# A hybrid decoder step on one Trainium2 core: expert 0 of each layer dispatched alone in the routing block, and one block from the experts to the attention values

## Chip, cores and metric

The kernel runs on one core of a Trainium2 chip, as one program and one launch. The metric is the device time of one execution in microseconds (us), the median of several. TensorE (PE in the profile) multiplies, PEld is its loading of stationary operands, VectorE is DVE, ScalarE is ACT, GpSimd is POOL, and SyncE is SP, which issues most of the transfers.

## The reference, cut to what matters

Two layers run over 264 tokens (256 of a prompt, 8 of a sample). Each has a mixer, then 32 experts of which every token uses two, then a gate term (PLE). After layer 0 the shared latents and rotary keys are computed from the same `h`.

```python
h = h + mixer(rmsnorm(h))                       # layer 0: convolution, layer 1: attention on the latents
x = rmsnorm(h)                                  # experts: top 2 of 32 by group and inner logits
hmid = silu(xblk @ w1[e]) * (xblk @ w3[e])      # w1, w3: 1024 x 512 each, float32
y[tokens] += (hmid @ w2[e]) * gate              # w2: 512 x 1024
h = h + sigmoid(rmsnorm(h) @ w_gate + b) * (p[i] @ w_proj)
# after layer 0 only
u = rmsnorm(h); c = rmsnorm(u @ w_dkv); k_pe = rope(u @ w_kr)
# layer 1's mixer
cq = rmsnorm(rmsnorm(h) @ w_dq); q = cq @ w_uq; k = c @ w_uk; v = c @ w_uv
```

All is float32. An expert's weights are 6 MiB (4 MiB for w1 and w3, which the kernel calls "up", and 2 MiB for w2, "down"); both layers together load 384 MiB of them.

## The kernel before, in words

`h` is held transposed as `hT` (8 chunks of 128 features by 264 tokens). The engines' programs are written out by hand, block by block; at the end of a block (`nc.Block()`) every engine waits for all others. Inside a block only semaphores order the work, and each engine runs its list in order.

`route_stage` (line 1033) is one block. It computes the logits, picks the experts, turns the tokens' rows into `u_rows` (tokens by features), counts ranks, and makes `sel`, one-hot columns that say which token sits in which slot. An expert has 32 slots. PE runs `busy`, products whose result nobody reads, where it would be idle. Then `dispatched` multiplies `u_rows` by `sel`, two feature chunks at a time (f = 0 to 3), which gives the inputs of experts 0 to 3 at once, transposed, and ACT copies them out with the gain (`dispatch_copy`).

`experts_stage` (line 1371) is the next block. It runs 36 turns, one for an expert (four experts have two). In turn e PE runs `expert_up` (line 1012, 32 products in four column groups), ACT the silu, DVE the product and a transpose (`turn_hidden`), PE `expert_down`, then ACT and DVE copy the result to `y`. Beside the turns stand the dispatch for the next eight turns (`fill_at`), `widen` (line 1541 on), `combine`, and from turn 32 on `project` of the PLE term. DVE has, ahead of turn 0, some 5 us of placing arithmetic (lines 1779 to 1809). The last combination, `combine_strips`, ends with eight additions to `hT`, from which ACT makes the eight gained chunks `uT`.

The weights lie in `area`: three up slots (`UPS`) and two down slots (`DOWNS`). Up slots 0 and 1 and both down slots are loaded long before; slot 2 at the start of `route_stage` (`first_up`). SP issues the up load of expert 3 once `up_done` of turn 0 is counted, that of expert 4 after turn 1, and so on; POOL issues nearly all down loads after `down_done`. From expert 4 on SP first reads the expert's number from memory (`expert_at`, line 1409).

`ple_stage` (line 1936) is the block after the experts. For each of 8 output chunks PE runs eight products of `uT` with the gate weights (line 1964) into PSUM banks 0 and 1 by turns; from chunk 2 on it waits for `scaled` of two chunks before. DVE needs the root of the sum of squares (lines 2046 to 2053) before it can scale. In layer 0 the next two blocks are `chunked` (line 2161) parts of `mla_stage` (line 2215): the latents, the rotary key and the down query, then keys, queries and values. In layer 1 `ple_stage` is the end, with turned rows (`followed`) between the products.

## Time and profile before

| | us |
|---|---|
| median of 3 runs (range) | 1435.5 (1432.87 to 1437.76) |
| the profiled execution, its own time | 1436.19 |
| its span in the trace | 1434.5 |
| PE busy | 1152.4 |
| DVE busy | 509.4 |
| ACT busy | 315.7 |

The times of rows below count from the start of the span; 1.7 us lie outside it. A row of the order in time gives start, duration, engine, line, operation, and in brackets how long the engine had been idle and what released it. Of a float32 product the trace counts two instructions.

### The profile page before, as it was taken

Reading aid. Unit: us, or ns where it says so; the run is one execution under the profiler, and the core shown is the slowest. Engines: PE = TensorE matmul, PEld = TensorE weight load, DVE = VectorE, ACT = ScalarE, POOL = GpSimd, SP = SyncE. Lnnn points to the kernel's source line nnn. Section 1 sums busy time; section 2 is a strip of 40 time slices with the busy share of each in tenths; the row PEclk is TensorE's granted clock in tenths of the full one; section 3 lists DMA queues with packets and bytes.
Section 4 is the critical chain, followed back from the end, with each engine's and each line's share of the span. In section 5 each row is a group of like instructions: output and inputs, shape, how many; then the busy total and the mean of one; then the engine's idle time right before and its main releaser. Section 6 shows DMA issues by size and latency. Waiting matters only on the chain. (4 is left out here: it accounts for less than half of the span.)

```text
span 1434.5 us, 25593 instructions
## 1 busy us (share of the span) xinstructions
PE 1152.4 (80%) x10905; PEld 726.7 (51%) x10905; DVE 509.4 (36%) x1421; ACT 315.7 (22%) x790; POOL 57.8 (4%) x84
## 2 busy tenths in 40 slices
PE   8999896857669676889989889997956958776687
PEld 7767653524325333467756557654533524333356
DVE  4873612212213121254856562522212212122144
ACT  4564320101101010142223330331100101101133
POOL 0200000000000000000011100000000000000000
PEclk9999997979879788999999999998988978889989
DMA  9453399999999999993033336679999999999970
GB/s 330 157 224 162 130 426 426 426 426 426 428 427 426 427 426 426 425 334 137 0 141 133 140 126 251 248 301 427 426 426 428 426 427 427 425 428 425 421 293 31
DMA packets 60235, 464.12 MB, mean 324 GB/s; under 512 B 17628, under 2 KB 28921, under 8 KB 33470
## 3 DMA queue, kind: packets, MB, share of 16 engines
q1 hardware_dynamic: 50974, 338.09, 57.6%
q0 software_dynamic: 8992, 123.74, 20.7%
q8 instruction: 90, 1.47, 0.4%
q10 hardware_dynamic: 144, 0.52, 0.1%
q14 instruction: 35, 0.29, 0.1%
HBM read 460.80 MB, written 2.49 MB: 323 GB/s over the span
## 5 line engine op out<-in xcount | busy, mean ns | idle before, releaser
L1018 PE MATMUL ps<-area,uT 128*32 128x256 f32 x2560 | 176.9, 437 | 95.7 <-DMA area<-in_w_exp_up_dram 93.5
L1018 PE MATMUL ps<-area,xsT 128*32 128x256 f32 x2048 | 152.7, 464 | 97.8 <-DMA area<-in_w_exp_up_dram 97.8
L1818 DVE TENSOR_TENSOR hidden<-silu,ps 128x128 f32<-128x128 f32 x72 | 20.7, 287 | 484.5 <-ACT silu L1678 484.5
L1018 PEld LDWEIGHTS ps<-area,uT 128*32 128x32 f32 x2560 | 91.7, 125 | 177.4 <-DMA area<-in_w_exp_up_dram 103.0
L1028 PE MATMUL ps<-area,hiddenT 128*32 128x256 f32 x2304 | 147.0, 398 | 26.0 <-issue 19.2
L1018 PEld LDWEIGHTS ps<-area,xsT 128*32 128x32 f32 x2048 | 76.1, 133 | 173.1 <-DMA area<-in_w_exp_up_dram 107.7
L1725 DVE COPY y<-ps 32x256 f32<-32x256 f32 x140 | 58.3, 416 | 192.8 <-PE ps L1028 191.0
L1349 PE MATMUL ps<-sel,u_rows 128*128 128x256 f32 (+3 forms) x480 | 124.6, 386 | 0.3
L1678 ACT ACTIVATE silu<-ps 128x128 f32<-128x128 f32 x72 | 20.0, 277 | 472.4 <-PE ps L1018 472.4
L1028 PEld LDWEIGHTS ps<-area,hiddenT 128*32 128x32 f32 x2304 | 71.6, 113 | 90.6 <-issue 37.2
L1349 PEld LDWEIGHTS ps<-sel,u_rows 128*128 128x128 f32 (+1 forms) x480 | 77.1, 187 | 44.5 <-issue 34.3
L1662 ACT COPY y<-ps 32x256 f32<-32x256 f32 x140 | 51.0, 365 | 159.2 <-PE ps L1028 158.3
L1526 PE MATMUL ps<-share,y 128*128 128x264 f32 (+1 forms) x288 | 83.9, 413 | 2.0 <-DVE hT L1708 1.5
L1964 PE MATMUL ps<-uT,area 128*128 128x264 f32 x256 | 63.2, 408 | 7.4 <-PEq L1453 7.4
L1526 PEld LDWEIGHTS ps<-share,y 128*128 128x128 f32 (+1 forms) x288 | 48.1, 189 | 37.3 <-issue 25.5
L320 PE MATMUL ps<-const,area 128*128 128x128 f32 (+2 forms) x356 | 55.3, 288 | 13.1 <-DVE cacheT L332 7.7
L1000 POOL DMA_DIRECT2D area<-in_w_exp_down_dram x50 | 26.7, 534 | 857.1 <-issue 644.8
L1964 PEld LDWEIGHTS ps<-uT,area 128*128 128x128 f32 x256 | 51.3, 203 | 17.6 <-issue 8.2
L1708 DVE TENSOR_TENSOR hT<-ps,hT 128x264 f32<-128x264 f32 x144 | 53.8, 409 | 5.7 <-PE ps L1526 5.6
L320 PEld LDWEIGHTS ps<-const,area 128*128 128x128 f32 (+2 forms) x356 | 40.7, 146 | 26.9 <-DVE cacheT L332 10.7
L590 PE MATMUL ps<-uT,area 128*128 128x264 f32 x160 | 36.6, 388 | 0.9 <-DVE conv_acc_sb L773 0.9
L590 PEld LDWEIGHTS ps<-uT,area 128*128 128x128 f32 x160 | 30.1, 190 | 6.7 <-DVE conv_acc_sb L773 1.3
(409 smaller groups left out, 1291.0 us busy)
## 6 DMA issues: line engine op xcount, KB each, us to landing
area<-in_w_exp_gate_dram SPq DMA_DIRECT2D x64, 2048.0 KB, 26.7
area<-in_w_exp_up_dram SPq DMA_DIRECT2D x64, 2048.0 KB, 33.6
area<-in_w_exp_down_dram POOLq DMA_DIRECT2D x50, 2048.0 KB, 15.3
area<-in_w_exp_down_dram SPq DMA_DIRECT2D x14, 2048.0 KB, 22.5
area<-in_conv_w_in_dram SPq DMA_DIRECT2D x8, 1024.0 KB, 21.5
area<-in_w_ple_gate_dram SPq DMA_DIRECT2D x8, 1024.0 KB, 20.8
area<-in_conv_w_out_dram SPq DMA_DIRECT2D x1, 4096.0 KB, 26.2
area<-in_w_o_dram SPq DMA_DIRECT2D x1, 4096.0 KB, 14.4
```

The lines of the kernel that those rows point to most:

```text
L320: last = pe.transpose(s.ps[0:m, 8 - banks + g % banks, at:at + n], src, col(s, "ident", slice(0, n))[:, 0:n])
L590: done = pe.matmul(s.ps[:, pair(m) + half, 0:T], w_in[:, k, a:a + P], s.uT[:, k, :], start=(k == 0), stop=(k == DC - 1))
L1000: engine.dma_start(down_view(s, slot).rearrange("p j d -> p (j d)"), src.rearrange("a p n -> (a p) n"))\
L1018: last = pe.matmul(s.ps[SLOT * j:SLOT * (j + 1), bank, 0:2 * P].rearrange("p (a f) -> p a f", a=2), xT[:, k, :], up[:, :, k, j * P:(j + 1) ...
L1028: last = pe.matmul(s.ps[SLOT * g:SLOT * (g + 1), bank, 0:q], hidden[:, SLOT * j:SLOT * (j + 1)], down[:, j, g * q:(g + 1) * q], start=(j = ...
L1349: last = pe.matmul(s.ps[:, bank, (c % 2) * WIDE + at:(c % 2 + 1) * WIDE], rows_of(m, t, c), m.sel[0:rows, t, at:WIDE], start=(t == 0), sto ...
L1526: pe.matmul(s.ps[:, 6 + c % 2, 0:T], y[0:rows, quad % 2, c * P:(c + 1) * P], share[0:rows, 0, :], start=True, stop=True).then_inc(s.comb_m ...
L1662: last = nc.scalar.copy(y[a:a + SLOT, (e // PER) % 2, g * q4:(g + 1) * q4], s.ps[SLOT * g:SLOT * (g + 1), 3 + e % 2, 0:q4])
L1708: V.tensor_tensor(s.hT[:, c, :], s.ps[:, 6 + c % 2, 0:T], s.hT[:, c, :], ALU.add)\
L1725: last = V.tensor_copy(y[a:a + SLOT, (e // PER) % 2, g * q4:(g + 1) * q4], s.ps[SLOT * g:SLOT * (g + 1), 3 + e % 2, 0:q4])
L1818: V.tensor_tensor(hid[:], act_out[:], s.ps[:, e % 2, P:2 * P], ALU.mult).then_inc(s.gated.sem, 1)
L1964: mm = pe.matmul(s.ps[:, c % 2, 0:T], w[:, k, c * P:(c + 1) * P], s.uT[:, k, :], start=(k == 0), stop=(k == DC - 1))
```

## The change

- **Expert 0 alone.** In `route_stage` DVE makes the 32 columns of `sel` for expert 0 first, then the other 96. PE multiplies them with `first_rows` (12 products in four column groups: rows of the slot by features), runs two fillers, and DVE transposes the result in 32 x 32 blocks and applies the gain. PE then runs `expert_up` of expert 0 in this block. SP waits there for it and issues the up load of expert 3. Only f = 0 of the dispatch of experts 1 to 3 (96 columns) is left in the block.
- **The first turns.** f = 1, 2 and 3 move to turn 0 of `experts_stage`; the dispatch for the next eight turns moves from turns 0 to 3 to `begun`, a turn or half a turn later. DVE's placing arithmetic now stands behind its first transpose, and its copy of turn 0 ahead of `choose(1)`.
- **One block.** `experts_stage`, `ple_stage` and, in layer 0, both `chunked` parts stand in one block. The barriers between them go, and waits on counts take their place. SP waits for the last `up_done` before the loads of attention weights, and for the end of the gate products before w_o.
- **Gate products.** They take the chunks of `uT` in the order in which these come, waiting for each, and use banks 0, 1, 5 and 7 (in layer 1 the second four use 0, 1, 0, 1). The product of the sum of squares moves from behind chunk 0 to behind chunk 1. `combine_strips` uses banks 2 to 7, so its last two products wait for an addition.
- **Latents.** Behind the last gate product PE runs seven of the eight products each for both latent chunks, the last sum of squares, and seven for the rotary key; the eighth of each follows once the last chunk is gained.
- Counters are merged (`conv_set`, `prepared`).

```diff
@@ route_stage
+                sp.wait_ge(s.up_done.sem, s.up_done.at(1))
+                first_up(sp, s, io, layer, UPS)
...
                 busy(pe, 2)
+                pe.wait_ge(s.first_sel.sem, s.first_sel.at(1))
+                first_rows(pe, s, m, 4).then_inc(s.first_mm.sem, 1)
+                busy(pe, 2)
+                pe.wait_ge(s.up_in[0].sem, s.up_in[0].at(32))
+                pe.wait_ge(s.first_out.sem, s.first_out.at(1))
+                expert_up(pe, s, up_view(s, 0), first_inputs(s)[:, :, P:P + SLOT], 0).then_inc(s.up_done.sem, 1)
                 pe.wait_ge(s.sel_ready.sem, s.sel_ready.at(1))
-                for f in range(DC // 2):
-                    if f >= 2:
-                        pe.wait_ge(s.xs_out.sem, s.xs_out.at(f - 1))
-                    dispatched(pe, s, m, f, 5 + f % 2, P).then_inc(s.xs_mm.sem, 1)
+                dispatched(pe, s, m, 0, 5, P + SLOT).then_inc(s.xs_mm.sem, 1)
...
+                own = first_inputs(s)[:, :, P:P + SLOT]
+                dve.wait_ge(s.first_mm.sem, s.first_mm.at(1))
+                link(V.transpose(own, s.ps[:, 4, 0:DC * SLOT].rearrange("p (k m) -> p k m", k=DC)))
+                V.tensor_tensor(own, own, s.gain[:, layer, :].rearrange("p (k a) -> p k a", a=1)
+                                .broadcast_to([P, DC, SLOT]), ALU.mult).then_inc(s.first_out.sem, 1)
@@ experts_stage
+        begun = {0: ((), ()), 1: ((), (0,)), 2: ((1,), (2,)), 3: ((3,), ())}
...
+            def dispatch_rest(f):
+                if f >= 2:
+                    pe.wait_ge(s.xs_out.sem, s.xs_out.at(f - 1))
+                dispatched(pe, s, m, f, 5 + f % 2, P + SLOT).then_inc(s.xs_mm.sem, 1)
...
-                for p in range(UPS, CUT):
+            for p in range(UPS + 1, CUT):
@@ ple_stage
+    banks = (0, 1, 5, 7, 0, 1, 0, 1) if last else (0, 1, 5, 7) * 2
...
+            for n, (k, gained) in enumerate(m.gained):
+                if c == 0:
+                    pe.wait_ge(s.gained.sem, gained)
+                mm = pe.matmul(s.ps[:, banks[c], 0:T], w[:, k, c * P:(c + 1) * P], s.uT[:, k, :],
+                               start=(n == 0), stop=(n == DC - 1))
@@ mla_stage
+            for b, (weights, a) in enumerate(firsts):
+                if weights is w.kr:
+                    last_sum(pe)
+                    pe.wait_ge(s.prepared.sem, s.prepared.at(1))
+                for k in range(DC - 1):
...
+            return "job", last_product, raw_result(raw, c)
```

Three places of PE's list follow; a name in brackets is a counter that the instruction waits for. The first is the end of `route_stage` and the start of the experts' block in layer 0. L1094 are fillers, L1349 the dispatch, L1018 the up products. Before:

```order
L1094 MATMUL ps<-hT,ones 128x264
L1349 MATMUL ps<-sel,u_rows 128x128 [waits sel_ready]
L1349 MATMUL ps<-sel,u_rows 128x128 x11
L1349 MATMUL ps<-sel,u_rows 128x128 [waits xs_out]
L1349 MATMUL ps<-sel,u_rows 128x128 x5
L1349 MATMUL ps<-sel,u_rows 128x128 [waits xs_out]
L1349 MATMUL ps<-sel,u_rows 128x128 x5
L1096 UNCONDITIONAL_BRANCH
L1507 UNCONDITIONAL_BRANCH [waits barrier_Pool_Activation_PE_DVE_SP_release]
L1018 MATMUL ps<-area,uT 32x256 [waits xs_out,up_in0]
```

After (L1375 is `first_rows`, L1364 the dispatch, L1028 the down products):

```order
L1094 MATMUL ps<-hT,ones 128x264
L1375 MATMUL ps<-u_rows,sel 32x256 [waits first_sel]
L1375 MATMUL ps<-u_rows,sel 32x256 x11
L1094 MATMUL ps<-hT,ones 128x264 x2
L1018 MATMUL ps<-area,uT 32x256 [waits first_out,up_in0]
L1018 MATMUL ps<-area,uT 32x256 x31
L1364 MATMUL ps<-sel,u_rows 128x96 [waits sel_ready]
L1364 MATMUL ps<-sel,u_rows 128x96 x5
L1096 UNCONDITIONAL_BRANCH
L1532 UNCONDITIONAL_BRANCH [waits barrier_Pool_Activation_PE_DVE_SP_release]
L1364 MATMUL ps<-sel,u_rows 128x96 x6
L1028 MATMUL ps<-area,hiddenT 32x256 [waits down_in0,h_ready]
```

The up products of expert 0 moved from behind 24 dispatch products and the barrier to ahead of both; eighteen of the dispatch products moved behind the barrier.

The second place is the end of layer 0's experts and the first gate products. Before (L1538 are the strips, L1964 the gate products, L1969 the sum of squares):

```order
L1538 MATMUL ps<-more_share,y 128x264 x7
L1453 UNCONDITIONAL_BRANCH
L1956 UNCONDITIONAL_BRANCH [waits barrier_Pool_Activation_PE_DVE_SP_release]
L1964 MATMUL ps<-uT,area 128x264 [waits ple_in0]
L1964 MATMUL ps<-uT,area 128x264 x7
L1969 MATMUL ps<-rstd,ones 128x264 [waits summed]
L1964 MATMUL ps<-uT,area 128x264 x8
L1964 MATMUL ps<-uT,area 128x264 [waits scaled,ple_in1]
```

After:

```order
L1570 MATMUL ps<-more_share,y 128x264 x5
L1570 MATMUL ps<-more_share,y 128x264 [waits added] x2
L2017 UNCONDITIONAL_BRANCH
L2027 MATMUL ps<-uT,area 128x264 [waits gained,ple_in0]
L2027 MATMUL ps<-uT,area 128x264 [waits gained] x7
L2027 MATMUL ps<-uT,area 128x264 x8
L2032 MATMUL ps<-rstd,ones 128x264 [waits summed]
L2027 MATMUL ps<-uT,area 128x264 [waits ple_in1]
L2027 MATMUL ps<-uT,area 128x264 x15
L2027 MATMUL ps<-uT,area 128x264 [waits scaled,ple_in2]
```

The barrier is gone, the products of chunk 0 wait for one gained chunk each, and two more chunks stand ahead of the first wait for `scaled`.

The third place is from the last gate products to the down query. Before (L2157 are the latents, the rotary key with 64 rows, and the down query):

```order
L1969 MATMUL ps<-area,ones 128x264 [waits summed]
L1969 MATMUL ps<-area,ones 128x264 [waits squared]
L1952 UNCONDITIONAL_BRANCH
L2181 UNCONDITIONAL_BRANCH [waits barrier_Pool_Activation_PE_DVE_SP_release]
L2157 MATMUL ps<-area 128x264 [waits attn_in0]
L2157 MATMUL ps<-area 128x264 x15
L2157 MATMUL ps<-area 64x264 [waits swapped]
L2157 MATMUL ps<-area 64x264 x7
L2157 MATMUL ps<-area 128x264 [waits proj_out,attn_in1]
```

After:

```order
L2409 MATMUL ps<-area 128x264 [waits gained,attn_in0,scaled]
L2409 MATMUL ps<-area 128x264 [waits gained] x6
L2409 MATMUL ps<-area 128x264 x7
L2394 MATMUL ps<-area,ones 128x264 [waits summed]
L2396 MATMUL ps<-area,ones 128x264 [waits squared]
L2409 MATMUL ps<-area 64x264 [waits prepared]
L2409 MATMUL ps<-area 64x264 x6
L2416 MATMUL ps<-area 128x264 [waits gained]
L2416 MATMUL ps<-area 128x264
L2416 MATMUL ps<-area 64x264
L2224 MATMUL ps<-area 128x264 [waits proj_out,attn_in1]
```

Fourteen products now stand ahead of the last sum of squares, and no barrier between.

## Rows read from the trace of the kernel before

**Rows 1.** The page, 40 slices: DMA's busy share in tenths, and GB/s

```profile
DMA  9453399999999999993033336679999999999970
GB/s 330 157 224 162 130 426 426 426 426 426 428 427 426 427 426 426 425 334 137 0 141 133 140 126 251 248 301 427 426 426 428 426 427 427 425 428 425 421 293 31
```

**Rows 2.** Who SP waited for: total us, times, longest

```profile
SPq L1409 <- PE ps L1018: 616.6, 48, 24.4
```

**Rows 3.** Order in time, layer 0: the end of routing and turn 0

```profile
160.60 1.13 PE L1094 MATMUL ps<-hT,ones 128*128 128x264 f32 x4 [0.99 <-ACT u_rows L1087]
...
161.57 8.49 PE L1349 MATMUL ps<-sel,u_rows 128*128 128x128 f32 x48
...
171.18 5.35 PE L1018 MATMUL ps<-area,uT 128*32 128x256 f32 x64 [1.12 <-PEq L1096]
...
176.58 0.33 SPq L994 DMA_DIRECT2D area<-in_w_exp_gate_dram  x1
...
177.22 0.41 DVE L1364 STREAM_TRANSPOSE hiddenT<-hidden 128x128 f32<-128x128 f32 x1
```

**Rows 4.** The same list in layer 1: the same load of expert 3

```profile
941.26 0.33 SPq L994 DMA_DIRECT2D area<-in_w_exp_gate_dram  x1
```

**Rows 5.** Two stretches: length, engines' busy us, granted clock, DMA share, GB/s

```profile
172.00:173.00 1.00, 1.00 (x19) 0.65 (x12) 0.83 (x6) 0.28 (x1) 0.00 (x0) 0.52 0.00 0
...
176.00:180.00 4.00, 2.72 (x45) 1.24 (x37) 3.31 (x12) 2.14 (x8) 0.04 (x1) 1.00 0.63 172
```

**Rows 6.** Order in time, layer 0: turns 0 and 1

```profile
177.68 1.93 PE L1028 MATMUL ps<-area,hiddenT 128*32 128x256 f32 x32 [1.15 <-DVE hiddenT L1364]
...
183.11 3.66 PE L1018 MATMUL ps<-area,uT 128*32 128x256 f32 x64
...
187.83 0.36 SPq L994 DMA_DIRECT2D area<-in_w_exp_gate_dram  x1
```

**Rows 7.** Order in time, layer 0: the last turns, the gate, the latents

```profile
596.65 6.34 PE L1018 MATMUL ps<-area,uT 128*32 128x256 f32 x64 [3.37 <-DMA area<-in_w_exp_up_dram]
...
619.89 1.17 PE L1538 MATMUL ps<-more_share,y 32*128 32x264 f32 x16 [0.54 <-DVE y L1721]
...
621.11 3.35 ACT L1699 ACTIVATE uT<-hT,vec 128x264 f32<-128x264 f32 x8 [1.32 <-DVE hT L1840]
...
624.77 6.10 PE L1964 MATMUL ps<-uT,area 128*128 128x264 f32 x16 [3.71 <-PEq L1453]
...
631.15 25.08 PE L1964 MATMUL ps<-uT,area 128*128 128x264 f32 x112
...
659.88 16.51 PE L2157 MATMUL ps<-area 128*128 128x264 f32 x64 [0.32 <-PEq L1952]
```

**Rows 8.** The first load of gate weights: issue, and time from issue to landing

```profile
L1920 SPq DMA_DIRECT2D area<-in_w_ple_gate_dram x1: 435/435/435, 591.7 to 591.7; - x1
...
DMA to landing us min/median/max: 27.4/27.4/27.4
```

**Rows 9.** Order in time, layer 0: the second sum, the latent norm, the first keys

```profile
658.85 0.71 PE L1969 MATMUL ps<-area,ones 128*128 128x264 f32 x2 [0.57 <-DVE area L2040]
...
676.23 1.05 PE L391 MATMUL ps<-latent_squares,ones 128*128 128x264 f32 x4
...
685.20 1.97 PE L2157 MATMUL ps<-cT,area 128*128 128x256 f32 x8 [0.79 <-PEq L2167]
```

**Rows 10.** Order in time, layer 1: the gate products of the end

```profile
1389.41 6.07 PE L1964 MATMUL ps<-uT,area 128*128 128x264 f32 x16 [3.71 <-PEq L1453]
...
1390.70 3.13 DVE L2046 TENSOR_TENSOR rstd<-rstd,area 128x264 f32<-128x264 f32 x6
...
1398.31 0.43 DVE L2053 TENSOR_TENSOR xsT<-ps,rstd 128x264 f32<-128x264 f32 x1
...
1400.26 0.52 ACT L2017 ACTIVATE area<-hT,vec 128x264 f32<-128x264 f32 x1 [0.97 <-DVE hT L2064]
...
1402.88 0.38 PE L1973 MATMUL ps<-const,area 128*128 128x128 f32 x2
```

More of the change, by code:

```diff
@@ L1351, in dispatched, with first_rows @@
     return last
+def first_rows(pe, s, m, bank):
+    for t, (_, rows) in enumerate(TILES):
+        for g in range(PER):
+            src = m.u_rows[0:rows, t, :].rearrange("t (k p) -> t k p", k=DC)[:, :, SLOT * g:SLOT * (g + 1)]
+            out = s.ps[SLOT * g:SLOT * (g + 1), bank, 0:DC * SLOT].rearrange("p (k m) -> p k m", k=DC)
+            last = pe.matmul(out, m.sel[0:rows, t, P:P + SLOT], src, start=(t == 0), stop=(t == 2))
+    return last
 def dispatch_copy(copy, s, layer, xT, f, bank, at=0):
```

1173 lines of the change are left out of this document (615 added, 558 removed).

## The prediction

> **What bounds the kernel now.** I read the page first. The slices of DMA show two long stretches near full (5 to 17 and 27 to 37 of 40) with a nearly empty stretch before each [rows 1]. Those are the experts. SP waited 616.6 us there in 48 waits for up products to free a slot [rows 2]; the slots are full, and behind them stands a queue of transfers. The last but one load of up weights still makes PE wait, at 596.65 [rows 7]. So each experts' stage lasts as long as its transfers, counted from their first issue, and that issue is what counts: SP may ask for expert 3 only when PE ends the up products of turn 0, at 176.58 in layer 0 [rows 3] and 941.26 in layer 1 [rows 4]. No transfer of weights runs before it. Around the experts PE's chain sets the time: 8 gate products of eight, the latents, the queries.
>
> **First part: the load of expert 3 is issued earlier.** PE's fillers before the dispatch end at 160.60 + 1.13 = 161.73 [rows 3]; the selection of expert 0 is a part of the old one and is ready by then. From there the new path is:
> - `first_rows`, 12 products in groups of four. Turn 1's up products, 32 of the same shape, take 3.66 us [rows 6], so a group of four takes 0.46, and 12 take 1.37: to 163.1.
> - DVE's transpose of 256 columns: 128 columns take 0.41 [rows 3], so between 0.41 and 0.82; I take 0.55. The multiplication by the gain is like the 0.43 of [rows 10]. With some 0.2 for hand-overs the inputs stand at 164.3. Two fillers (half of 1.13, 0.6 to 1.1 with their start) hide part of it from PE's clock.
> - the up products at the full clock, 3.66: to 168.0, and the issue at 168.05.
>
> That is 8.5 us before 176.58. DVE's waits and two operations (2.9 us in all) stand ahead of the rest of its routing arithmetic, but ACT's copy of the dispatch ends the block before: PE dispatches f = 0 now until about 170.1, as f = 3 before (161.57 + 8.49 = 170.06 [rows 3]), so the next block still starts near 171.2.
>
> **What comes late next** is the load of expert 4, issued after turn 1's up products. Ahead of these PE has, from 171.2: the dispatch f = 1, turn 0's down products (1.93 [rows 6]), f = 2 and 3, and turn 1's 3.66. A dispatch of 128 columns costs 8.49 / 4 = 2.12 [rows 3]; with 96 columns at least three quarters of that, 1.59, at most all; I take 1.9. Sum 5.7 + 1.93 + 3.66 + 0.3 of waits = 11.6: to 182.8. In before PE's clock was granted at half (0.52 in 172 to 173 [rows 5]), after the barrier's 1.12 us of idling, and turn 0 took 5.35 instead of 3.66. That barrier stays, so I add the same 1.7: to 184.5. SP issues 1.06 after the products' end, since it must read the expert's number (183.11 + 3.66 = 186.77 against 187.83 [rows 6]): 185.6.
> The transfers ahead of it are expert 3 up (4 MiB) and a down load (2 MiB), 6.29 MB. After the issue at 176.58 the stretch 176 to 180 moved 4.0 us x 172 GB/s = 0.69 MB, 1.6 us at the 426 GB/s of the page's slices [rows 1]; so data flow 1.8 after the issue [rows 5]. The queue is then empty at 168.05 + 1.8 + 14.8 = 184.65, and expert 4 flows from 187.4. **The hole is 2.75**, and 1.05 without the low clock. Later issues come before the queue runs dry (expert 5's near 196.9, when expert 4 and a down load keep it until 202.3). So a layer's experts end 8.5 - 2.75 = 5.75 earlier, and two layers give **11.5** (bounds: a hole of 4 each, 9.0; a hole of 1.05, 14.9). DVE's placing arithmetic, now behind turn 0's transpose, ends near 179; the next reader of `sel` for turns 4 on needs it at 188.
>
> On the clock: the row shows the level fall to 1.2 GHz after a gap of 1.12 us [rows 3, 5]. The Trainium skill, "TensorE: Matmul & The Clock Gate", section "Loop structure matters more than you think", says that a short copy by DVE between batches of products doesn't cost the clock. By that rule the hole would be 1.05 and the two layers would give 14.9; by the row 11.5. I keep the row.
>
> **The gate in layer 0.** PE idled 3.71 from the strips to 624.77, and the first 8 products took 6.10 where later ones take 25.08 / 7 = 3.58 [rows 7]. Now they may start with the first gained chunk, at 621.11 + 0.42 + 0.1 = 621.65; ACT makes a chunk in 0.42, PE needs 0.45 for a product, so PE is not held up. The weights land at 591.7 + 27.4 = 619.1, 2.5 before [rows 8] (both move with the stream). Eight chunks and the sum at full clock: 8 x 3.58 + 0.7 = 29.3, to 651.0, against 631.15 + 25.08 = 656.23 [rows 7]: 5.2. With as much low clock as before, 2.5 less. No wait for `scaled` bites, since four banks let PE run ahead of the root. The strips' last two products wait for an addition each, 0.5 us later, hidden by DVE's own eight additions. I take **4.4** (2.7 to 5.2).
>
> **The latents.** From the end of the gate to the end of the first down query took 676.23 - 656.23 = 20.0 [rows 7, 9]. Now: 14 products at 0.448 (6.3), the sum (0.7, its last square is ready at 656.23 - 651.0 before 658.85, so at 653.6), 7 and 3 products (4.5), 8 of the down query (3.6), waits 0.4: 15.5. That gives 4.5. The root (two hand-overs and DVE's reciprocal) hides behind the rotary key's seven. The barrier before the keys goes too, and DVE's apply then limits them: 0.7 more. **5.2** (3.0 to 6.3; the low end if ACT's and DVE's results follow as late as before).
>
> **The gate in layer 1.** Here the rows of the result need the gained chunk 0, so the root counts. The running sum is ready at 1390.70 + 3.13 = 1393.83; PE made its product only behind the first, slow chunk, 1389.41 + 6.07 = 1395.48 [rows 10]. Now it comes at 1393.9 at the earliest, 1.6 sooner, and chunk 0 is gained at 1400.26 + 0.52 - 1.6 = 1399.2, when the turned rows go out, instead of 1402.88: 3.7. With a low clock in the first chunk the sum waits for PE again, and 2.2 is left. I take **2.9** (1 to 3.7).
>
> **The sum.** 11.5 + 4.4 + 5.2 + 2.9 = 24.0. The profiled execution took 1436.19, 0.7 above the median of the runs; 1436.2 - 24.0 = 1412.2, and in terms of the median 1411.5.
>
> **The rivals.**
> - The clock holds at turn 0 in both layers, and at the gate. For it: two fillers and the early up products keep PE busy to 168. Against: the same barrier stands behind the dispatch [rows 3, 5]. 14.9 + 5.2 + 5.2 + 3.7 = 29.0: 1406.5. Chance 0.22.
> - The start is given back. PE is the slower one in turns 0 to 4, and the queue could run dry again at turn 2 or 3, until only the old schedule is left; that decides if expert 5's load is issued after 202.3, 5.4 later than I put it. The stream then gives nothing: 24.0 - 11.5 = 12.5, 1423.0. Chance 0.08.
> - The merged blocks don't do what they say, since ACT and DVE, not PE, set the pace of gate and latents: 7 less, 1418.5. The rows with PE without a pause for 25.08 us speak against. Chance 0.05.
> - Slower: PE, waiting chunk by chunk for ACT, stays at half clock in the gates. A chunk then costs 6.10 instead of 3.58 [rows 7]; all 16 cost 16 x 2.5 = 40, time 1411.5 + 40 = 1451.5, and from ten such chunks on the change loses. Against it: today only the first chunk of eight is slow, and the second already costs 3.58. Chance 0.03.
> - Gains under 4.3 us for causes I don't see: 0.02.
>
> **How the numbers follow.** My forecast, 1411.5, has 0.60. The range takes in the clock that holds, both ends of the unknown costs, and the slower merged blocks, but not the stream that gives all back: 1404 to 1420. A measurement of this kernel tells 0.3% (4.3 us) from no change. All cases but the last two are faster by more: faster 0.95, same 0.02, slower 0.03.
>
> **What would show it.** In the changed profile: the load of expert 3 issued at 168.05 in layer 0, 8.5 earlier; a dip of DMA of about 3 us, some 17 after it; expert 4's issue near 185.6; the gate products starting 0.5 after the first gained chunk; no idle PE between gate and latents. I am wrong if the clock doesn't fall behind the barrier, if `first_rows` doesn't run four at a time (1.37 would be up to 5.5, and the stream lose 4 per layer), or if the queue has a second dip.

## The result, and the profile after

The changed kernel takes 1418.85 us in the median of four runs (1414.27 to 1424.74), the kernel before 1434.87; the ratio is 0.9879, 95% interval 0.9848 to 0.9911. Measured once more (e1) it is 1419.68 in six runs (1408.75 to 1423.67), ratio 0.9886 (0.9850 to 0.9922). The forecast was 1411.5, in a range of 1404 to 1420: the sign and the range hold, but the gain is 16, not 24. The profiled execution was the longest of the four, 1424.74 with a span of 1423.1; the profiled one of e1 took 1418.4 (span 1416.6) and lies near the median, so both are used.

The page of the changed kernel, DMA's busy share and GB/s (to be set beside [rows 1]):

```profile
DMA  9454589999999999994034427589999999999980
GB/s 331 159 218 172 199 362 427 426 427 426 427 427 424 428 426 424 426 332 181 1 142 143 152 108 287 223 321 426 427 427 426 426 426 427 426 427 425 426 306 31
```

The slice ahead of the first experts' weights, the fifth, had 130 GB/s and now has 199, and the next one has 362 where it had 426: weights flow earlier, and then stop for a while. In slices 25 to 27 of the second layer it is 287, 223, 321, where before had 251, 248, 301.

Order in time, layer 0, from expert 0's own inputs to the load of expert 4 (beside [rows 3] and [rows 6]):

```profile
163.00 1.64 PE L1375 MATMUL ps<-u_rows,sel 128*32 128x256 f32 x24
...
164.70 0.45 DVE L1262 STREAM_TRANSPOSE uT<-ps 128x256 f32<-128x256 f32 x1 [0.96 <-PE ps L1375]
165.18 0.42 DVE L1263 TENSOR_TENSOR uT<-uT,gain 128x256 f32<-128x256 f32 x1
...
165.75 3.66 PE L1018 MATMUL ps<-area,uT 128*32 128x256 f32 x64
...
169.34 2.07 PE L1364 MATMUL ps<-sel,u_rows 128*128 128x96 f32 x12
169.46 0.33 SPq L994 DMA_DIRECT2D area<-in_w_exp_gate_dram  x1
...
172.33 3.21 PE L1364 MATMUL ps<-sel,u_rows 128*128 128x96 f32 x12 [0.92 <-PEq L1096]
...
175.47 3.64 PE L1028 MATMUL ps<-area,hiddenT 128*32 128x256 f32 x32
...
179.04 4.54 PE L1364 MATMUL ps<-sel,u_rows 128*128 128x96 f32 x24
...
183.51 5.05 PE L1018 MATMUL ps<-area,uT 128*32 128x256 f32 x64
...
189.64 0.36 SPq L994 DMA_DIRECT2D area<-in_w_exp_gate_dram  x1
```

Down to the load of expert 3 the intervals are as forecast: it is issued 17.96 us after that of slot 2 (151.50), against 26.42 before, 8.46 earlier. Then PE is slow. The down products take 3.64 instead of 1.93, turn 1's up products 5.05 instead of 3.66, and expert 4's load comes 20.2 after expert 3's, where I had put 17.6. (The trace holds two entries for each of these products; counts here are of entries.) The windows of that stretch (length, busy us of PE, PEld, DVE, ACT, POOL, granted clock, DMA share, GB/s):

```profile
172.00:174.00 2.00, 1.67 (x7) 1.35 (x8) 0.10 (x1) 1.59 (x3) 0.00 (x0) 0.68 0.96 410
174.00:178.00 4.00, 4.00 (x30) 2.31 (x33) 3.59 (x16) 2.10 (x8) 0.00 (x0) 0.50 1.00 430
...
180.00:182.00 2.00, 2.00 (x13) 1.62 (x13) 0.54 (x2) 0.57 (x2) 0.18 (x1) 1.00 0.99 352
...
183.00:186.00 3.00, 3.00 (x26) 1.53 (x30) 2.15 (x6) 0.57 (x2) 0.00 (x0) 0.50 0.98 393
...
188.00:190.00 2.00, 2.00 (x22) 1.42 (x14) 0.69 (x2) 0.28 (x1) 0.00 (x0) 1.00 0.04 16
```

The clock falls twice. The first fall, at the barrier's pause, was forecast. The second comes at 183, while PE has worked without a pause since 172.3: what it did just ahead of it were the dispatch products of 96 columns. At 188 to 190 no weights flow (16 GB/s): that is the hole. In layer 1 the level stays at 1.2 GHz from 926.5 to 944:

```profile
926.00 2.74 PE L1364 MATMUL ps<-sel,u_rows 128*128 128x96 f32 x12 [0.92 <-PEq L1096]
928.67 3.64 PE L1028 MATMUL ps<-area,hiddenT 128*32 128x256 f32 x32
932.24 7.14 PE L1364 MATMUL ps<-sel,u_rows 128*128 128x96 f32 x24
939.31 6.03 PE L1018 MATMUL ps<-area,uT 128*32 128x256 f32 x64
```

and expert 4's load comes 23.2 after expert 3's.

The gate and the latents in layer 0 (beside [rows 7] and [rows 9]):

```profile
617.22 2.28 PE L1570 MATMUL ps<-more_share,y 32*128 32x264 f32 x16 [0.54 <-DVE y L1767]
619.42 9.07 PE L2027 MATMUL ps<-uT,area 128*128 128x264 f32 x32
628.34 0.61 PE L2032 MATMUL ps<-rstd,ones 128*128 128x264 f32 x2
628.78 21.52 PE L2027 MATMUL ps<-uT,area 128*128 128x264 f32 x96
650.14 6.39 PE L2409 MATMUL ps<-area 128*128 128x264 f32 x28
...
665.95 1.05 PE L391 MATMUL ps<-latent_squares,ones 128*128 128x264 f32 x4
```

PE has no pause in it, the first gate product follows right on the strips, 1.0 behind the start of the first gained chunk (618.43), and from the gate's end (650.30) to the sum of the latents' squares it is 15.65 instead of 20.0.

**Where the time is.** The span cut at the same ten marks, one profiled execution of each kernel, in us. "Stream" is from the issue of expert 3's load to the start of the last down products. It is 440.1 to 440.9 in the kernels below whose transfers do not stop once they flow (before, e7, e9).

| stretch | before | after | e1 | e3 | e6 | e7 | e9 | e8 |
|---|---|---|---|---|---|---|---|---|
| start to slot 2's load, layer 0 | 150.16 | 151.50 | 151.86 | 150.13 | 152.26 | 151.99 | 150.38 | 150.45 |
| to expert 3's load | 26.42 | 17.96 | 17.96 | 17.96 | 17.97 | 18.35 | 26.27 | 17.97 |
| stream, layer 0 | 440.84 | 445.28 | 445.33 | 444.08 | 443.29 | 440.15 | 440.85 | 442.22 |
| strips to the gate's end | 36.34 | 33.08 | 33.09 | 31.40 | 31.40 | 31.40 | 31.40 | 31.40 |
| gate's end to the queries' products | 39.94 | 34.67 | 34.73 | 34.63 | 34.56 | 34.71 | 34.55 | 39.24 |
| to slot 2's load, layer 1 | 218.68 | 220.20 | 219.27 | 220.33 | 223.09 | 223.51 | 220.24 | 218.01 |
| to expert 3's load | 26.41 | 17.96 | 17.97 | 17.97 | 17.97 | 18.35 | 24.74 | 17.97 |
| stream, layer 1 | 440.79 | 449.34 | 443.29 | 443.99 | 441.58 | 440.13 | 440.44 | 442.80 |
| strips to the end, layer 1 | 49.97 | 48.15 | 48.15 | 46.49 | 46.45 | 46.49 | 46.08 | 47.80 |
| span (with 2.5 twice from last down to strips) | 1434.5 | 1423.1 | 1416.6 | 1411.9 | 1413.5 | 1410.0 | 1419.9 | 1412.8 |

The width of the hole can be read from the bytes. In the 20 us that begin 10 us behind the issue of expert 3's load the kernel before moves 428 GB/s, in layer 0 and much the same in layer 1 (430); a full slice of its page has 426. Less than that in the same stretch, turned into time, is the hole:

| layers 0 and 1 | after | e1 | e3 | e6 | e7 | e8 |
|---|---|---|---|---|---|---|
| GB/s | 313, 245 | 311, 375 | 333, 339 | 384, 390 | 421, 418 | 378, 380 |
| hole, us | 5.3, 8.5 | 5.4, 2.4 | 4.4, 4.1 | 2.0, 1.7 | 0.2, 0.4 | 2.3, 2.2 |
| expert 3's load to expert 4's | 20.2, 23.2 | 20.2, 17.2 | 19.0, 18.9 | 16.6, 16.5 | 7.3, 7.3 | 17.1, 17.0 |

In every column but e7's, where the second load comes in time, the hole is 14.6 to 14.9 less than the time between the two loads. The stream rows differ from these by up to 1.1, as PE's clock at the last turns is in them too.

The first and the sixth row, whose work the change leaves as it was, differ by up to 2.1 and 5.5 between the kernels; for instance 16 products at L856 took 5.40 in the changed kernel and 3.83 in before. Before has nearly the shortest of both, but e8, which is the changed kernel in both stretches, has 150.45 and 218.01: the difference belongs to the single execution, and it makes a single pair of profiles uncertain by some us. Single runs of the changed kernel spread over 16 us (ten runs), those of e3 over 3 (six), those of the kernel before over 12 (23 runs beside e1).

### The profile page after: what moved, and what is told of

It reads as the page before. It is cut to its first block and busy times, and to the rows that moved or that the text cites. A ratio compares the mean times of both kernels' runs of the same rounds, so it can differ in the third digit from the quotient of the medians.

```text
span 1423.1 us, 25682 instructions
## 1 busy us (share of the span) xinstructions
PE 1170.9 (82%) x10961; PEld 739.8 (52%) x10961; DVE 512.0 (36%) x1437; ACT 315.0 (22%) x790; POOL 58.0 (4%) x84
## 5 line engine op out<-in xcount | busy, mean ns | idle before, releaser
L1018 PE MATMUL ps<-area,uT 128*32 128x256 f32 x2560 | 182.9, 447 | 96.2 <-DMA area<-in_w_exp_up_dram 93.8
L1018 PE MATMUL ps<-area,xsT 128*32 128x256 f32 x2048 | 147.3, 451 | 87.0 <-DMA area<-in_w_exp_up_dram 87.0
L1018 PEld LDWEIGHTS ps<-area,uT 128*32 128x32 f32 x2560 | 92.1, 128 | 183.1 <-DMA area<-in_w_exp_up_dram 102.9
L1028 PE MATMUL ps<-area,hiddenT 128*32 128x256 f32 x2304 | 148.5, 401 | 18.4 <-issue 13.7
L1018 PEld LDWEIGHTS ps<-area,xsT 128*32 128x32 f32 x2048 | 75.2, 129 | 156.8 <-DMA area<-in_w_exp_up_dram 95.4
L1364 PE MATMUL ps<-sel,u_rows 128*128 128x256 f32 (+3 forms) x480 | 129.3, 398 | 1.8 <-PEq L1096 1.8
L1028 PEld LDWEIGHTS ps<-area,hiddenT 128*32 128x32 f32 x2304 | 71.7, 114 | 84.6 <-issue 33.9
L1364 PEld LDWEIGHTS ps<-sel,u_rows 128*128 128x128 f32 (+1 forms) x480 | 81.3, 198 | 47.8 <-issue 41.6
L2027 PEld LDWEIGHTS ps<-uT,area 128*128 128x128 f32 x256 | 50.3, 199 | 9.8 <-issue 0.7
```

The costliest lines, as they stand in the source:

```text
L1018: last = pe.matmul(s.ps[SLOT * j:SLOT * (j + 1), bank, 0:2 * P].rearrange("p (a f) -> p a f", a=2), xT[:, k, :], up[:, :, k, j * P:(j + 1) ...
L1028: last = pe.matmul(s.ps[SLOT * g:SLOT * (g + 1), bank, 0:q], hidden[:, SLOT * j:SLOT * (j + 1)], down[:, j, g * q:(g + 1) * q], start=(j = ...
L1364: last = pe.matmul(s.ps[:, bank, (c % 2) * WIDE + at:(c % 2 + 1) * WIDE], rows_of(m, t, c), m.sel[0:rows, t, at:WIDE], start=(t == 0), sto ...
L2027: mm = pe.matmul(s.ps[:, banks[c], 0:T], w[:, k, c * P:(c + 1) * P], s.uT[:, k, :], start=(n == 0), stop=(n == DC - 1))
```

## The experiments

The theories. The hole in the stream is what part one loses. **A**: it is as wide as it is since products of 96 columns hold PE at half clock. **B**: the pause at the barrier does it. **C**: it differs with the single execution.

**e1: the changed kernel again**, no edit.

> The changed kernel once more, nothing edited. Its first profile came from the slowest of four executions (1424.7 of 1414.3 to 1424.7), and there the clock was granted at half for 14 of the first 15 us of turns 0 and 1 in layer 1 (926.5 to 944) and for about 11 in layer 0. Theory A (the half clock follows from what PE executes there, products of 96 columns): the long half clock returns in this profile, expert 4's load is again issued 19 to 24 us after expert 3's in both layers, and the median stays at 1416 to 1421. Theory C (it is a matter of the single execution): another profile shows half clock for 4 us or less behind the barrier, expert 4's load 17 to 18 us after expert 3's, and a time of 1414 or less for that execution.

Measured: 1419.68. Layer 0 is the same to 0.05 us (20.18 between the loads, stream 445.33). In layer 1 the level was low for some 3 us only (the down products took 3.36, turn 1's up products 3.66) and the loads came 17.18 apart, stream 443.29 instead of 449.34. So C has a part: the same code costs 6 us more in one execution than in another. Even so a hole of 2.4 remains.

**e3: the dispatch at its full width.**

```diff
-                dispatched(pe, s, m, f, 5 + f % 2, P + SLOT).then_inc(s.xs_mm.sem, 1)
+                dispatched(pe, s, m, f, 5 + f % 2, P).then_inc(s.xs_mm.sem, 1)
...
-                dispatched(pe, s, m, 0, 5, P + SLOT).then_inc(s.xs_mm.sem, 1)
+                dispatched(pe, s, m, 0, 5, P).then_inc(s.xs_mm.sem, 1)
```

> One size changed: the dispatch products of experts 1 to 3 take all 128 columns of the group, not 96 (the 32 more are computed and not copied). Theory A (products of 96 columns behind weights of 128 keep PE at half clock or throw it back there, with no pause of PE needed): the second fall of the clock (at 183 in layer 0) goes away, the level returns to full within 4 us of the barrier in both layers, expert 4's load comes 16.5 to 18 us after expert 3's instead of 20.2 and 23.2, and the kernel is 4 to 9 us faster than the changed one. Theory B (the 0.92 us pause at the barrier and the waits for ACT's copies behind it do it): nothing changes, within 2 us of the changed kernel, half clock as long as in it. At full clock the wider products cost at most 0.005 us each more (8.49/48 = 0.177 against 2.07/12 = 0.173).

Measured: 1415.02 (1413.64 to 1416.74), ratio 0.9864 (0.9839 to 0.9889), 4.7 less than e1 on the same chip, though the two intervals overlap. PE in layer 0, behind the barrier:

```profile
171.07 3.09 PE L1364 MATMUL ps<-sel,u_rows 128*128 128x128 f32 x12 [0.92 <-PEq L1096]
174.09 3.64 PE L1028 MATMUL ps<-area,hiddenT 128*32 128x256 f32 x32
177.66 4.80 PE L1364 MATMUL ps<-sel,u_rows 128*128 128x128 f32 x24
182.39 3.66 PE L1018 MATMUL ps<-area,uT 128*32 128x256 f32 x64
```

The second fall is gone (3.66, not 5.05); the first is there still (3.09, 3.64). The loads are 19.0 and 18.9 apart, not the 16.5 to 18 expected, so A could be right on the second fall alone. The wider products cost next to nothing: 2.18 for 12 against 2.07.

But e8, described below, has the same narrow dispatch as the changed kernel, and its profile has no second fall either:

```profile
171.29 2.32 PE L1364 MATMUL ps<-sel,u_rows 128*128 128x96 f32 x12 [0.92 <-PEq L1096]
173.63 3.24 PE L1028 MATMUL ps<-area,hiddenT 128*32 128x256 f32 x32
176.80 4.08 PE L1364 MATMUL ps<-sel,u_rows 128*128 128x96 f32 x24
180.81 3.66 PE L1018 MATMUL ps<-area,uT 128*32 128x256 f32 x64
```

In its layer 1 it is the same (4.08, 3.66). So of the six layers profiled with 96 columns (after, e1, e8) three had turn 1's up products slow, and of the six with 128 columns behind one early expert (e3, e6, e11) none. That speaks for A and does not prove it: with so few layers C could do as much. The gate was faster by 1.7 in each layer of e3: its first 32 products take 7.39 where the changed kernel had 9.07 in both profiles and both layers. That is not the dispatch's width either: e8's layer 0 has 7.39 with 96 columns, and e5's layer 1 has 9.07 with 128. What the level does at the gate is open.

**e4: 96 columns in the kernel before.** In the routing block's dispatch `P` becomes `P + SLOT`, the columns of expert 0 are not computed.

> The kernel before with the 48 dispatch products of its routing block cut from 128 columns to 96; the columns of expert 0 are left out, so its inputs are not computed. No pause, wait or barrier is added. Theory A: the level falls to half inside these products, which ran at the full level for 8.5 us in before, and they take 10 to 16 us; the kernel is 2 to 8 us per layer slower, though it computes less. Theory B: the level stays full, the products take 8.2 to 8.4, and the time is within 2 us of before.

Measured: 1443.12 (1439.11 to 1445.73), ratio 1.0055 (1.0038 to 1.0073): a quarter of the dispatch left out makes the kernel slower. Expert 0's inputs are then missing, so what follows computes with other values. The 48 products took 14.04 in layer 0 and 11.13 in layer 1, against 8.49. In layer 1, where the level was full at their start (the windows' seventh number is the clock):

```profile
931.82 11.13 PE L1349 MATMUL ps<-sel,u_rows 128*128 128x96 f32 x48
...
934.00:936.00 2.00, 2.00 (x13) 1.62 (x13) 1.83 (x11) 0.62 (x3) 0.00 (x0) 0.94 0.00 0
936.00:938.00 2.00, 2.00 (x8) 1.66 (x9) 1.40 (x7) 0.54 (x2) 0.00 (x0) 0.50 0.00 0
```

PE has no pause from 931.8 on, and its level falls at 936. In before the 48 products of 128 columns ran at 2.4 GHz from first to last. That shows A's mechanism by itself. In layer 0 the level had fallen ahead of them, at 161, and did not come back in 14 us of such products. In layer 0 of e9 the level fell at the same place, and behind it stood the 128 columns:

```profile
160.82 2.06 PE L1094 MATMUL ps<-hT,ones 128*128 128x264 f32 x4 [0.99 <-ACT u_rows L1087]
162.67 9.14 PE L1348 MATMUL ps<-sel,u_rows 128*128 128x128 f32 x48
172.93 3.66 PE L1018 MATMUL ps<-area,uT 128*32 128x256 f32 x64 [1.12 <-PEq L1096]
```

There the level was back at 165, and the 48 cost 9.14. So the width matters; by e8 it does not decide every time.

**e6: fillers at the barrier**, on e3.

```diff
                 dispatched(pe, s, m, 0, 5, P).then_inc(s.xs_mm.sem, 1)
+                busy(pe, 2)
```

> e3_wide_rest with two filler products behind the last dispatch of the routing block, so that PE works while ACT copies and the barrier comes: its pause shrinks from 0.92 us to about 0.4. Theory B1 (the pause at the barrier starts the low clock): the level stays full behind the barrier, turn 0's down products take 1.93 instead of 3.64, expert 4's load comes 15.5 to 16.5 us after expert 3's instead of 19.0, and the kernel is 4 to 7 us faster than e3. Rival (the fall comes anyway, from the dispatch products or from the change of work): half clock behind the barrier as in e3, same time within 2 us.

Measured: 1413.50 (1410.76 to 1415.31), ratio 0.9840 (0.9816 to 0.9865).

```profile
173.68 2.15 PE L1365 MATMUL ps<-sel,u_rows 128*128 128x128 f32 x12 [0.30 <-PEq L1096]
176.02 1.93 PE L1028 MATMUL ps<-area,hiddenT 128*32 128x256 f32 x32 [0.19 <-DVE hiddenT L1390]
177.89 4.29 PE L1365 MATMUL ps<-sel,u_rows 128*128 128x128 f32 x24
182.11 3.66 PE L1018 MATMUL ps<-area,uT 128*32 128x256 f32 x64
```

B holds for the first fall: with a pause of 0.30 instead of 0.92 the level stays at 2.4 GHz, and the loads come 16.6 apart. It is so in all six layers with these fillers (e6, e10, e12), and in all ten with the pause of 0.92 (after, e1, e3, e8, e11) the level fell behind it. The fillers both shorten the pause and put wide products ahead of it; which of the two keeps the level isn't told apart. The time moved only 1.5 from e3, within the spread, where I had expected 4 to 7. The hole did get 2.4 narrower in both layers, by the bytes. In e6's profile this is lost again elsewhere: 4.9 in the first and sixth rows, and 1.7 in layer 0's last up products, which ran at half clock (5.35) and so are in its stream row. The rule of the Trainium skill, "TensorE: Matmul & The Clock Gate", section "Loop structure matters more than you think", which I had set against this row, speaks of a copy by VectorE between batches of products. The wait of 0.19 for VectorE's transpose, through which the level stayed, agrees with it; the 0.92 at the barrier lies outside it.

**e7: experts 0 and 1 both alone**, on e3. Three places of it:

```diff
-                first = select(nc, s, m.sel[:, :, P:P + SLOT], early_rel, 0, P)
+                first = select(nc, s, m.sel[:, :, P:P + 2 * SLOT], early_rel, 0, P)
...
                 first_rows(pe, s, m, 4).then_inc(s.first_mm.sem, 1)
-                busy(pe, 2)
+                first_rows(pe, s, m, 7, 1).then_inc(s.first_mm.sem, 1)
...
                 expert_up(pe, s, up_view(s, 0), first_inputs(s)[:, :, P:P + SLOT], 0).then_inc(s.up_done.sem, 1)
+                pe.wait_ge(s.up_in[1].sem, s.up_in[1].at(32))
+                pe.wait_ge(s.first_out.sem, s.first_out.at(2))
+                expert_up(pe, s, up_view(s, 1), first_inputs(s)[:, :, P + SLOT:P + 2 * SLOT], 1).then_inc(s.up_done.sem, 1)
...
-        begun = {0: ((), ()), 1: ((), (0,)), 2: ((1,), (2,)), 3: ((3,), ())}
+        begun = {0: ((), ()), 1: ((), ()), 2: ((0,), (1,)), 3: ((2,), (3,))}
```

> A candidate on top of e3_wide_rest: experts 0 and 1 are both dispatched alone with products of four a time (the second 24 take the place of the two fillers) and both have their up products ahead of the barrier; the first dispatch products of the second group stand behind turn 2's up products, not turn 1's down. If the hole in the stream of weights is what keeps part one from its gain (5.5 and 6.4 us without transfers in the first profile, some 4 in e3), expert 4's load now comes 7 to 9 us after expert 3's, the hole behind expert 3 is gone in both layers, and the kernel is 5 to 9 us faster than e3, 1406 to 1410. If the stream then runs dry one turn later (expert 5's load more than 25 us after expert 3's), the gain is 0 to 3.

Measured: 1408.00 (1406.67 to 1411.92), ratio 0.9810 (0.9785 to 0.9835). It beats both kernels of the case.

```profile
163.49 3.20 PE L1381 MATMUL ps<-u_rows,sel 128*32 128x256 f32 x48
166.62 7.11 PE L1018 MATMUL ps<-area,uT 128*32 128x256 f32 x128
...
176.70 3.53 PE L1370 MATMUL ps<-sel,u_rows 128*128 128x128 f32 x12 [0.86 <-PEq L1096]
```

Expert 4's load is issued 7.3 after expert 3's, and the stream is 440.15 and 440.13: no hole to speak of, though the clock falls at the barrier as before (3.53 for 12 products) and expert 5's load comes 21 later. With the queue full PE's clock in turns 0 to 2 costs nothing. That shows that part one lost most of its gain in the hole.

**e2, e5 and e9: part one undone, three times.** e9 is part two alone; e2 and e5 are on the way to it and failed to be that, each by the place of one piece of VectorE's work. e2 puts the dispatch of experts 0 to 3 back in front of the barrier, with the up products of expert 0 in turn 0:

```diff
-                pe.wait_ge(s.first_sel.sem, s.first_sel.at(1))
-                first_rows(pe, s, m, 4).then_inc(s.first_mm.sem, 1)
...
+                for f in range(DC // 2):
...
+                    dispatched(pe, s, m, f, 5 + f % 2, P).then_inc(s.xs_mm.sem, 1)
```

> The first part undone in the changed kernel: expert 0 is dispatched with experts 1 to 3 again (48 products of 128 columns ahead of the barrier, up products of expert 0 in turn 0, load of expert 3 behind them). All that concerns gate, latents and keys stays changed. As predicted blind (part one is worth 11.5): 11 to 12 us slower than the changed kernel, near 1430. By the profile of the changed kernel (stream gained 4.0 in layer 0 and nothing in layer 1): 3 to 6 us slower, 1422 to 1425, and only 10 to 13 faster than before, all of it from gates and latents.

Measured: 1438.24 (1431.71 to 1445.34), ratio 1.0026 (1.0004 to 1.0048), slower than before. Both forecasts missed, since the undoing was not clean: `place()` stood behind turn 0's transpose, where the changed kernel has it, and the selection of the next group behind that.

> As e2_group_of_four, with one thing more: VectorE computes the places of the tokens in front of turn 0's work, beside its up products, as in the kernel before, so that the selection for the second group doesn't come late. In e2 PE waited 6.10 us for that selection behind turn 0's down products and was at half clock after it. Expected: that wait is gone, expert 4's load comes some 11 us after expert 3's as in before (e2: 21.5), and what is left is part two alone. By the rows of the first profile (gate 3.2, latents and keys 5.3, gate of layer 1 1.8) 10 us faster than before, 1424; by the blind numbers 12.5, 1422. If e2's loss had another cause, it stays near 1438.

Measured: 1432.45 (1427.82 to 1438.30), ratio 0.9986 (0.9968 to 1.0004). `place()` was in front again, but the selection still behind the copy of turn 0's outputs. The first dispatch of the next group, in e2 and in e5:

```profile
184.15 6.37 PE L1348 MATMUL ps<-sel,u_rows 128*128 128x256 f32 x12 [6.10 <-DVE sel L1320]
```

```profile
184.38 6.38 PE L1348 MATMUL ps<-sel,u_rows 128*128 128x256 f32 x12 [3.06 <-DVE sel L1320]
```

A wait of 6.10 or 3.06 for VectorE, and both times half clock behind it (6.37 for 3.44), with expert 4's load 21.5 and 18.8 behind expert 3's.

```diff
-                    copy_out(0)
                     choose(1)
+                    copy_out(0)
```

> As e5_part_two_alone with one order mended: behind turn 0 VectorE makes the selection of the second group before it copies turn 0's outputs, as in the kernel before (in e5 it came behind the copy and PE waited 3.06 us for it, then ran the next dispatch at half clock, 6.38 for 3.44). This is now part two alone. Expected: expert 4's load 11.2 us after expert 3's as in before, stretch from expert 3's load to the last down products 440.8 us as in before, and a time of 1423 to 1425 (10.4 to 12.5 less than before). Part one is then worth 3 to 6 as it stands in the changed kernel (1419). Rival: part two costs something in the experts' stage itself (merged block, placing arithmetic), and the time stays at 1430 or more.

Measured: 1422.83 (1418.15 to 1426.75), ratio 0.9902 (0.9872 to 0.9932), and stream 440.85 and 440.44. So part two alone is worth some 13.5, and part one, as the change has it, 1 to 3 more, which these intervals don't separate from nothing. With 128 columns (e3) it is worth some 6, with two experts alone (e7) some 13. These are differences of gains, each gain taken against the kernel before as measured beside it (medians 1434.38 to 1436.28). One thing in e9's profile is luck of the clock: turn 0's up products behind the barrier took 3.66 in both layers, where before they took 5.35, which makes layer 1's way to expert 3's load 24.74 instead of 26.41. e5, with the same code there, had 5.35 in both.

**e8: the latents undivided**, behind the second sum.

```diff
-                for k in range(DC - 1):
...
-                    pe.matmul(s.ps[0:min(P, weights.shape[2]), b, 0:T], weights[:, k, a:a + min(P, weights.shape[2])],
...
+            return dense(pe, s, b, weights, a, min(P, weights.shape[2]), v.latent_in, DC)
```

> One part undone in the changed kernel: the products of the latents and of the rotary key stand undivided behind the second sum, instead of seven of each eight ahead of it; the joined block stays. The sum of squares is ready only 2.6 us after the gate's last product by the blind working, and the root takes until some 4.5 after it, while the first drawn-forward products take 6.3. Expected: 2 to 4 us slower than the changed kernel (PE idles between gate and latents for 1.5 to 3), the rest of the 5.3 of latents and keys comes from the barriers that went. Rival: it is within 0.5 us, because ACT's and VectorE's results set the pace in any case.

Measured: 1421.40 (1414.77 to 1425.21), ratio 0.9903 (0.9877 to 0.9929), beside e1's 1419.68 and 0.9886, which the intervals don't separate. The profile is sharper:

```profile
645.92 0.68 PE L2394 MATMUL ps<-area,ones 128*128 128x264 f32 x2 [1.42 <-DVE area L2123]
647.11 1.03 PE L2396 MATMUL ps<-area,ones 128*128 128x264 f32 x2 [0.50 <-DVE area L2103]
647.94 16.16 PE L2224 MATMUL ps<-area 128*128 128x264 f32 x64
```

The gate ends at 644.50, the latents' squares are summed at 663.93: 19.4 against 15.65. Up to these squares drawing the products forward is worth 3.8 of the 4.35 gained; it fills the two waits of 1.42 and 0.50, and fewer products are left behind them. Up to the queries' products it is 4.6 (39.24 against 34.67) of 5.3, of which 0.8 is four products at a lower clock (2.07 for 1.28).

**e11: the gate waits for all its inputs**, on e3.

```diff
-                if c == 0:
-                    pe.wait_ge(s.gained.sem, gained)
+                if c == 0 and n == 0:
+                    pe.wait_ge(s.gained.sem, m.gained[-1][1])
+                    pe.wait_ge(s.squares_act.sem, s.squares_act.at(1))
```

> On e3_wide_rest, one thing undone: the first gate product waits for all eight gained chunks and the first square, which is where the barrier stood in before; all else stays joined. The chunks take ACT 3.36 us, the first product starts 0.9 after the first of them begins. Expected: PE idles 2.5 to 3 us ahead of the gate in both layers, and by the first profile's half clock behind such a pause the first chunk or two cost 1.5 to 2.5 more; the way from the strips to the gate's end in layer 0 grows from 31.4 to 34 to 36.3, layer 1's from the strips to the end from 46.5 to 49 to 50; in all 5 to 8 us slower than e3. Rival (ACT and VectorE set the pace of the gate): less than 2.

Measured: 1424.34 (1423.41 to 1426.80), ratio 0.9918 (0.9890 to 0.9945): the gain on the kernel before is 11.9, where e3's is 19.5.

```profile
620.67 9.45 PE L2028 MATMUL ps<-uT,area 128*128 128x264 f32 x32 [2.74 <-ACT area L2071]
```

A pause of 2.74 and 2.1 of half clock behind it: from the strips (615.65) to the gate's end (651.92) it is 36.3, as in before (36.34), and 31.4 in e3. In layer 1 it is 50.3 from the strips to the end, against 46.5. So the start with the first gained chunk is worth 4.9 and 3.8 against e3; 2.7 of each is the pause, and the rest the clock behind.

**e10 and e12: further on e7.** e10 has e6's fillers, and the product of the gate's first sum behind the second product of chunk 1:

```diff
+                if c == 1 and n == 2:
+                    pe.wait_ge(s.summed.sem, s.summed.at(DC - 1))
+                    sum_of(s.rstd[:], True, True).then_inc(s.sums.sem, 1)
```

> e7_two_alone with two fillers behind the last dispatch of the routing block (as in e6) and with the product of the first sum of squares behind the second product of gate chunk 1, not behind the chunk. In layer 1 of the changed kernel PE waited 1.35 us for gained chunk 0 behind chunk 2, since the sum came 2.2 after the running sum was ready. Expected: that wait goes (1.3 us less in layer 1, nothing in layer 0), the stream is unchanged (the fillers only keep the clock), and the kernel is 1 to 3 us faster than e7, 1405 to 1407. If the clock in turns 0 to 2 matters in e7 beyond the stream, 3 to 5.

Measured: 1411.46 (1406.89 to 1412.99), ratio 0.9818 (0.9789 to 0.9846). The sum in layer 1:

```profile
1370.61 1.12 PE L2044 MATMUL ps<-rstd,ones 128*128 128x264 f32 x2 [2.01 <-DVE rstd L2118]
```

I had taken the place from the changed kernel's profile, where the gate ran at half clock. At the full clock PE is there 2.01 too early; it waits, and is at half clock behind it. From the strips to the end layer 1 takes 48.4, not 46.5, and layer 0's gate 34.0, not 31.4. e12 takes the moved sum out again.

> e10 without its moved sum, that is e7_two_alone with two fillers behind the routing block's last dispatch. In e10 PE came to the moved sum 2.01 us too early, waited, and was at half clock behind it, so that layer 1 took 48.4 us from the strips to the end, against 46.5 in e7. Expected: that way is 46.5 again, layer 0's gate 31.4; the stream from expert 3's load to the last down products stays at 440 in both layers, since e7 had no hole left to close; time 1406 to 1409, equal to e7 within 2 us. If the fillers' full clock in turn 0 were worth something beyond the stream, 1403 to 1406.

Measured: 1408.02 (1405.48 to 1412.63), ratio 0.9822 (0.9803 to 0.9841), 46.5 in that stretch: no difference to e7 that the intervals show, so the fillers give nothing measurable once the queue is full.

## Why the prediction was right, and where it fell short

**The first issue, 8.5 earlier: right.** 8.46 in both layers. `first_rows` took 1.64 for my 1.37 (0.137 for one product, not 0.114), the transpose 0.45 for 0.55, the product with the gain 0.42 for 0.43.

**The issue of expert 4: the term that was too small.** I had 17.55 between the loads. Measured were 20.2 and 23.2 in the changed kernel, 20.2 and 17.2 in e1, 17.1 and 17.0 in e8, which has the same code there. Two terms are in it. "I take 1.9" for 12 products of 96 columns: they take 2.07 at the full clock and 12 of 128 take 2.18, so a quarter of the columns less saves 0.11; the loads of their weights span 1.91 of the 2.07, which suggests that these set it. And "so I add the same 1.7" for the low clock. Added up over the products from the barrier to turn 1's last up product, against their times at the full clock, it cost 4.7 and 7.8 in the changed kernel, 4.7 and 1.4 in e1, 1.6 and 1.6 in e8. So 1.7 is what it is when the level falls once and comes back in some 3 us; in the changed kernel it stayed down for 6 us and fell again without a pause, or stayed down for 17. I had taken one level and one length for what has several. With 128 columns (e3, e11) the cost was 1.6 to 3.2 and no second fall came. e4 and e9 show that narrow products can hold the level down or throw it down; which of the cases comes in a given execution stays open.

**The hole, 2.75 in each layer: too small.** By the bytes it is 5.3 and 8.5 in the changed kernel, 5.4 and 2.4 in e1, 2.3 and 2.2 in e8. The working of it was right: the 6.29 MB ahead of expert 4 last 14.8, and the measured time between the two loads less 14.8 (20.2, 20.2, 23.2 and 17.2) gives the measured holes to 0.1. So the miss is in the issue, and its size goes with the level: where that fell once, for some 3 us (e8), the hole is even below my 2.75. The stretch from slot 2's load to the last down products gained 4.0 and -0.1 in the profiled execution, 4.0 and 5.9 in e1's, and not 5.75 twice. My bound of 4 for the hole was no bound. e7 takes the hole out and gets 8.7 in each layer, no less than the 8.1 by which its issue is earlier.

**The gate of layer 0: right.** Taken 4.4 (2.7 to 5.2), between a full and a low clock; measured 3.3 with 9.07 for the first 32 products, and 4.9 wherever they took 7.39 (e3, e6, e7, e8, e9). e11 shows the mechanism.

**Latents and keys: right.** Taken 5.2, measured 5.3: 4.35 up to the latents' squares (I had 4.5) and 0.9 behind them (I had 0.7). e8 puts 3.8 of the 4.35 on the products drawn forward. The 0.9 I put down to the barrier before the keys, where PE had idled 0.79; no run has that barrier alone.

**The gate of layer 1: right in kind.** Taken 2.9 (1 to 3.7), measured 1.8, or 3.5 at the full clock. One step was wrong: I let the sum come as soon as its input is ready, 1.6 sooner. The change has it behind chunk 1:

```profile
1380.71 3.12 DVE L2109 TENSOR_TENSOR rstd<-rstd,area 128x264 f32<-128x264 f32 x6
...
1386.07 0.61 PE L2032 MATMUL ps<-rstd,ones 128*128 128x264 f32 x2
...
1391.58 0.44 PE L2036 MATMUL ps<-const,area 128*128 128x128 f32 x2 [1.35 <-ACT area L2080]
```

The running sum is ready at 1383.83, its product comes at 1386.07, and PE waits 1.35 for the gained chunk in the end.

**The sum.** 24.0 forecast; by the table 11.4 in the profiled execution: 3.9 of stream for 11.5, 3.3 for 4.4, 5.3 for 5.2, 1.8 for 2.9, and 2.9 lost in stretches that the change doesn't touch. In e1's profile it is 17.9, with 9.9 of stream and 2.3 lost so. ("Stream" here is with the earlier issue.) The medians say 16 and 15. That they lie inside 1404 to 1420 owes something to luck: the upper end stood for merged blocks that are slower, which did not come, and not for a wider hole, whose bound would have given 1414.

**The rivals.** "The clock holds" (0.22) did not come; e6 is near to what it would have been, and gives 1413.5, not 1406.5. Its rows gain 27.5 where I had 29.0, with holes of 2.0 and 1.7 for my 1.05; but 6.5 are lost in the first and sixth rows. "The start is given back" (0.08) came in part, and by a way that I had not put there: not a second dip, but a wider first one, in layer 1 of one profile as wide as the whole gain. "Half clock in the gates" was priced at 40 for all 16 chunks; it came for a part of the first two, 1.7 in each layer. The merged blocks did what they say.

## What to carry to other kernels

When transfers are the bound and their first issue is moved, the gain is the smaller of two things: how much earlier the first comes, and how late the next is allowed to be. Work out the second with PE's products at either level of its clock, and if the queue runs dry at one of them, bring a second load forward too (e7: some 13 us, where one load alone gave 1 to 7). Don't cut columns from products whose weights take as long to load as the product: it saves next to nothing at the full clock and can cost the clock (e4). When an experiment undoes a part, look first whether its waits are those of the kernel before; e2 and e5 missed that by the place of VectorE's work, worth some 17 and 12 us against e9. And look at every profile that has the code in question, not only at those taken for it: e8 was made for the latents, and showed that the second fall does not always come.

## What the runs showed of the hardware

- TensorE's clock fell from 2.4 to 1.2 GHz while PE worked without a pause, on products of 96 columns behind weights of 128 (layer 1 of e4: at 936, 4 us into them; layer 0 of the changed kernel: at 183). The same products at 128 columns kept it for 8.5 us, and cost 0.18 each against 0.17. In e8 and in layer 1 of e1 the 96 columns of turn 0 did not throw it down a second time.
- A pause of 0.92 at a barrier cost the level in ten layers of ten, one of 0.30 with fillers ahead of it in none of six (e6, e10, e12), nor did the 0.19 behind it. The length alone does not decide: 1.12 at the barrier, with the same 48 products ahead, cost it in before and e5 (5.35 behind it) and not in e2 and e9 (3.66), and 1.16 ahead of the last down products cost nothing (1.93).
- Behind a pause of 3.06 and 6.10 the next 12 products of 256 columns took 6.38 and 6.37 instead of 3.44 (e5, e2): the length of the pause made no difference to these twelve.
- One kernel's executions differ by up to 15 us (1408.75 to 1423.67 in e1). Between the two profiles of the changed kernel 6.0 of 6.5 are one stream, by the clock in turns 0 and 1. Six runs of e3 stay within 3.1, but the kernel before, with 128 columns too, spreads over 12, so the width is not shown to be the reason.
